# Input projections in three f32r passes over rounded high and low parts, in units of 128 columns, with spilled features and alternating heads

## The reference

```python
h_lat = modulate(rmsnorm(x_lat, norm_mix_g[l]), mod[0], mod[1])     # h_ctx alike
# layer 0, even_mixer
z = h_lat @ w_in                        # (1024 x 3104): bg cg xa q g | k v lr_f lr_b
la_f = log_sigmoid(lr_f @ decay_up[0] + decay_b[0]) / GLA_TAU       # la_b alike
o, _, _ = gla_bidir(q * scale, k, v, la_f, la_b, s_f, s_b)          # 4 heads, chunks of 64
conv = dwconv(cg * xa, conv_w, conv_b, 1)
y = concatenate([bg * conv, gla_readout(o, g, norm_g)]) @ w_out
# layer 1, odd_mixer
xb, gb, u, v = split(h_lat @ w_in)      # 4 x 512 columns
xc = dwconv(xb, conv_w, conv_b, 2)      # then two gates, and a scan in either direction
y = concatenate([(h_f + h_b) * gelu(gb), gelu(u) * mixed(layernorm(gelu(v)))]) @ w_out
# both layers
x = x + mod[2] * y;  x = x + mod[5] * ec_moe(modulate(rmsnorm(x, norm_ffn_g[l]), mod[3], mod[4]))
```

## Time and profile before

| | us |
|---|---|
| median of the runs | 2886.24 (2885.51 to 2896.28, 3 runs) |
| profiled execution | 2893.62 |
| its span | 2891.9 |
| TensorE busy | 2593.5 (90%) |
| VectorE busy | 1715.7 (59%) |
| ScalarE busy | 1364.0 (47%) |
| mean granted TensorE clock | 0.92 |

### The profile page before, as it was taken

How to read it: one execution, slowest core, us unless ns; L and a number is a source line. 1 busy time by engine, 2 the same in 40 slices (tenths; PEclk the granted TensorE clock), 3 DMA queues, 4 the chain that set the end, 5 groups by cost and what they waited for, 6 DMA issues and landing times.

```text
span 2891.9 us, 30954 instructions
## 1 busy us (share of the span) xinstructions
PE 2593.5 (90%) x11696; PEld 1733.4 (60%) x11696; DVE 1715.7 (59%) x1903; ACT 1364.0 (47%) x1371; POOL 182.6 (6%) x210
## 2 busy tenths in 40 slices
PE   4999999888897699999999995999888399999995
PEld 2444445476584366666666664544467278888884
DVE  3130020333456488888888873354554799999995
ACT  4210000144452466666666654155434277777774
POOL 0000000000000110101111000000000001111100
PEclk6899999877897799999999996999998699999997
DMA  6003332200246477878787874101134399999995
GB/s 223 29 0 116 116 115 89 73 16 1 88 175 230 173 270 288 301 280 306 281 308 280 292 251 133 44 0 44 58 132 167 130 361 388 392 391 391 391 376 200
DMA packets 164503, 571.02 MB, mean 197 GB/s; under 512 B 13640, under 2 KB 36928, under 8 KB 158272
## 3 DMA queue, kind: packets, MB, share of 16 engines
q1 hardware_dynamic: 153664, 532.07, 49.0%
q0 software_dynamic: 10752, 37.75, 5.2%
HBM read 527.84 MB, written 41.94 MB: 197 GB/s over the span
## 4 chain that ended last, share of the span: by engine, by line
PE 84%; DVE 6%; DMA 4%; ACT 3%; issue 1%; SPq 0%; POOL 0%; POOLq 0%; ACTq 0%; DVEq 0%
PE ps L541 17%; PE ps L1391 13%; PE ps L1392 12%; PE ps L1393 12%; PE ps L1404 6%; PE ps L551 4%; PE ps L682 3%; PE ps L743 2%; PE ps L745 2%; PE ps L744 2%; PE ps L472 1%; DMA R_W<-in_ada_w 1%; PE ps L758 1%; PE ps L1412 1%; PE ps L1476 1%
## 5 line engine op out<-in xcount | busy, mean ns | idle before, releaser
L1603 DVE TENSOR_TENSOR R_H_r<-R_M,R_W_r 128x2048 fp32r<-128x2048 f32 x336 | 761.8, 2289 | 147.2 <-ACT R_W_r L1506 146.9
L1506 ACT CAST R_W_r<-R_M 128x2048 fp32r<-128x2048 f32 x336 | 640.3, 1913 | 221.2 <-PE ps L1393 82.5
L1393 PE MATMUL ps<-R_W_r,R_C_r 128*128 128x512 f32 x1536 | 607.4, 395 | 0.0
L541 PE MATMUL ps<-R_H,R_W 128*128 128x512 f32 (+1 forms) x1408 | 533.6, 539 | 2.1 <-ACT R_W L1894 1.3
L541 PEld LDWEIGHTS ps<-R_H,R_W 128*128 128x128 f32 x1408 | 267.8, 191 | 273.1 <-issue 256.0
L1391 PE MATMUL ps<-R_W_r,bc_r 128*128 128x512 f32 x1024 | 413.4, 404 | 13.0 <-DVE R_C_r L1621 9.5
L1392 PE MATMUL ps<-R_H_r,bc_r 128*128 128x512 f32 x1024 | 405.8, 396 | 0.0
L1393 PEld LDWEIGHTS ps<-R_W_r,R_C_r 128*128 128x128 f32 x1536 | 291.3, 190 | 65.5
L1391 PEld LDWEIGHTS ps<-R_W_r,bc_r 128*128 128x128 f32 x1024 | 194.1, 190 | 70.7 <-issue 16.4
L1392 PEld LDWEIGHTS ps<-R_H_r,bc_r 128*128 128x128 f32 x1024 | 194.3, 190 | 41.5
L1391 PE MATMUL ps<-R_W_r,R_M_r 128*128 128x512 f32 x512 | 202.6, 396 | 7.0 <-DVE R_C L1693 4.6
(11 more groups left out here) (253 smaller groups left out, 2886.4 us busy)
## 6 DMA issues: line engine op xcount, KB each, us to landing
R_M<-in_moe_w_gate SPq DMA_DIRECT2D x114, 1024.0 KB, 7.9
R_M<-in_moe_w_down SPq DMA_DIRECT2D x112, 1024.0 KB, 7.3
R_M<-in_moe_w_up SPq DMA_DIRECT2D x110, 1024.0 KB, 7.3
R_W<-in_ada_w SPq DMA_DIRECT2D x48, 1024.0 KB, 6.6
R_H<-in_moe_w_up SPq DMA_DIRECT2D x18, 1024.0 KB, 9.5
R_H<-in_moe_w_down SPq DMA_DIRECT2D x16, 1024.0 KB, 9.9
R_H<-in_moe_w_gate SPq DMA_DIRECT2D x14, 1024.0 KB, 9.5
R_W<-in_ev_w_in SPq DMA_DIRECT2D x12, 1024.0 KB, 7.0
```

What stands on the lines that cost most here:

```text
L541: ins = pe.matmul(wide(j % 2, n)[:, c0:c0 + cn], w[:, k, half * P:(half + 1) * P], hT[:, k, c0:c0 + cn], start=(k == 0), stop=(k == KC - 1))
L1393: ins = pe.matmul(o, lo[:, k, 0:P], wh[:, kk, cs], start=False, stop=(k == KC - 1))
L1506: nc.scalar.copy(whi[j], raw[slot + j]).then_inc(unit_high_done, 1)
L1603: nc.vector.tensor_tensor(wlo[j], raw[slot + j], whi[j], ALU.subtract).then_inc(unit_low_done, 1)
```

## The change

Both layers' input projections now run as the output projection does. ScalarE copies a weight unit of 128 columns into f32r (`act_weight_high`), VectorE subtracts that from the raw one in place (`dve_weight_low`). h is modulated and rounded by ScalarE into R_H (`act_h_high`), and VectorE computes it again and subtracts (`dve_h_low`), so its low part stands in R_C. A job is then three f32r matmuls for each k and stretch. R_C being taken, the finished features (bg, g) go into scratch rows and from there to DRAM on GpSimd's queue, and come back as a whole after the last job.

What comes with it: v is made in two halves of 256 columns; the low-rank job is an ordinary job on 128 columns; the first eight ada units go into seven slots in R_M and are computed between the norm's transposes, x is loaded on ScalarE's queue into R_H at once, and the norm writes unmodulated copies of 512 columns. The other 24 ada units of the stage use one slot, two to a job, behind its first and second stretch. The order of the 18 late jobs becomes cg, xa, bg, twice, g, q. The exps and decays of head pair 0 stand ahead of the last jobs. In the attention, the loop over the heads is the inner one. In layer 1, gb goes to `bc` and u to the ends of R_H and R_C, the gate weights are loaded per channel group by ScalarE, and `fill` has 16 half tiles. The MoE and the output projection keep their instructions.

```diff
+        raw_at = [0, PIECE, 2 * PIECE, 6 * PIECE]
+        high_at = [3 * PIECE, 4 * PIECE, 5 * PIECE, 7 * PIECE]
+        wraw = [R_W[:, a:a + PIECE] for a in raw_at]
+        whigh = [R_Wr[:, a:a + PIECE] for a in high_at]
+        wlow = [R_Wr[:, a:a + PIECE] for a in raw_at]
...
+        even_units = [("lr", E_LR + 2 * RANK - P, 0), ("k0", E_K, 1), ("k1", E_K + P, 2), ("v3", E_V + 3 * P, 3),
+                      ("v0", E_V, 0), ("v1", E_V + P, 1), ("v2", E_V + 2 * P, 2)]
+        even_late = [(n, h + i, c + (h + i) * P) for h in (0, 2) for n, c in (("cg", E_CG), ("xa", E_XA), ("bg", E_BG)) for i in range(2)]
+        even_late += [("g", i, E_G + i * P) for i in range(4)] + [("q", i, E_Q + i * P) for i in range(2)]
+        even_units += [(f"{n}{b}", col, i % 3) for i, (n, b, col) in enumerate(even_late)]
+        odd_units = [("xb0", O_XB, 0), ("xb1", O_XB + P, 1), ("xb2", O_XB + 2 * P, 2), ("xb3", O_XB + 3 * P, 0),
...
+            group, place = i // 6, 2 * (i % 6) + part
+            if place < KC:
+                return "unit", N_FIRST + KC * group + place
+            return ("rows", 1 + group) if place == 9 else (None, None)
...
+        fill = [[("v", i) for i in range(6)], [("v", 6), ("v", 7), ("gb", 0)],
+                [("v", i) for i in range(8, 14)], [("v", 14), ("v", 15), ("gb", 1)],
+                [("gb", 2)], [("gb", 3), ("u", 0)], [("u", 1)], [("u", 2), ("u", 3)]]
...
+        split_behind = {("xb", 0): ["xb3"], ("xb", 1): ["w0"], ("xb", 2): ["w1"], ("xb", 3): ["gb0"], ("v", 7): ["w2", "w3"],
+                        ("gb", 0): ["gb1"], ("v", 15): ["gb2", "gb3"], ("gb", 1): ["u0"], ("gb", 2): ["u1"],
+                        ("gb", 3): ["u2"], ("u", 0): ["u3"]}
...
-            unit_in(pe, i)
-            w = ring[slot_of[i]].rearrange("p (k n) -> p k n", k=KC)
-            for c0, cn in SPLIT:
+            pe.wait_ge(weight_low_done, u + 1)
+            wh = whigh[slot_of[u]].rearrange("p (k n) -> p k n", k=KC)
+            wl = wlow[slot_of[u]].rearrange("p (k n) -> p k n", k=KC)
+            for part, (c0, cn) in enumerate(SPLIT):
                 if c0 >= n:
                     break
+                o = wide(j % 2, n)[:, c0:c0 + cn]
                 for k in range(KC):
-                    ins = pe.matmul(wide(j % 2, n)[:, c0:c0 + cn], w[:, k, half * P:(half + 1) * P],
-                                    hT[:, k, c0:c0 + cn], start=(k == 0), stop=(k == KC - 1))
+                    if h_from is not None:
+                        pe.wait_ge(h_low_done, h_from + KC * part + k + 1)
+                    pe.matmul(o, wh[:, k, :], tokens_of(R_Hr, k, c0, cn), start=(k == 0), stop=False)
+                    pe.matmul(o, wh[:, k, :], tokens_of(R_Cr, k, c0, cn), start=False, stop=False)
+                    ins = pe.matmul(o, wl[:, k, :], tokens_of(R_Hr, k, c0, cn), start=False, stop=(k == KC - 1))
+                if part < 2 and beside is not None:
+                    what, at = gap_ada(beside, part)
+                    if what == "unit":
+                        if at == N_FIRST:
+                            pe.wait_ge(v_tile_copied, 2 * NT)
+                        ada(pe, at)
+                    elif what == "rows":
+                        ada_rows(pe, at)
             ins.then_inc(job_done, 1)
...
+            vh, vl = pair_of(high_at, s), pair_of(raw_at, s)
+            o = ps[:, 6 + x % 2, 0:256].rearrange("p (u n) -> p u n", u=2)
             for k in range(KC):
-                ins = pe.matmul(out_, hT[:, k, t * P:(t + 1) * P], v2[:, k, :, :],
-                                start=(k == 0), stop=(k == KC - 1))
+                xh, xl = tokens_of(R_Hr, k, t * P, P), tokens_of(R_Cr, k, t * P, P)
+                pe.matmul(o, xh, vh[:, k, :, :], start=(k == 0), stop=False)
+                pe.matmul(o, xh, vl[:, k, :, :], start=False, stop=False)
+                ins = pe.matmul(o, xl, vh[:, k, :, :], start=False, stop=(k == KC - 1))
...
             for t in range(NT):
                 norm_transposes(pe, t, 2 * (t % 2), t - 2 if t >= 2 else None)
+                if t < N_FIRST:
+                    ada(pe, t)
+            ada_rows(pe, 0)
...
+            for j in range(3):
+                job(pe, j, j, h_from=0 if j == 0 else None)
+            j = 3
...
+            for x in range(2 * NT):
+                half, t = divmod(x, NT)
+                if t == 0:
+                    pe.wait_ge(weight_low_done, max(index["v0"], index["v1"]) + 1 if half == 0 else index["v2"] + 1)
+                if x >= 2:
+                    pe.wait_ge(v_tile_copied, x - 1)
+                v_tile(pe, x, t, 2 * half)
+            for i in range(len(even_late)):
+                job(pe, j, index["cg0"] + i, beside=i)
+                j += 1
             assert j == n_even_jobs
...
-                    for hh in range(2):
-                        for r in range(2):
-                            for tt in range(2):
+                    for r in range(2):
+                        for tt in range(2):
+                            for hh in range(2):
...
-                    for hh in range(2):
-                        for tt in range(2):
-                            t = 2 * g + tt
-                            o = ps[:, 6 + hh, tt * P:(tt + 1) * P]
-                            vh = vtok[:, t, (2 * p + hh) * P:(2 * p + hh + 1) * P]
-                            mm = [(o, vh, attS[:, n % 2, r, (2 * hh + tt) * P:(2 * hh + tt + 1) * P]) for r in range(2)]
-                            for r in range(2):
-                                for cc in range(2):
-                                    c = 2 * t + cc
-                                    if c != order[r][0]:
-                                        qd = (qT if r == 0 else kT)[64 * hh:64 * hh + 64, p, c * 64:(c + 1) * 64]
-                                        mm.append((o[:, cc * 64:(cc + 1) * 64], SIN[64 * hh:64 * hh + 64, r, c, :], qd))
-                            for x, (oo, lhs, rhs) in enumerate(mm):
-                                ins = pe.matmul(oo, lhs, rhs, start=(x == 0), stop=(x == len(mm) - 1))
+                    for tt in range(2):
+                        t = 2 * g + tt
+                        for r in range(2):
+                            for hh in range(2):
+                                pe.matmul(ps[:, 6 + hh, tt * P:(tt + 1) * P],
+                                          vtok[:, t, (2 * p + hh) * P:(2 * p + hh + 1) * P],
+                                          attS[:, n % 2, r, (2 * hh + tt) * P:(2 * hh + tt + 1) * P],
+                                          start=(tt == 0 and r == 0), stop=False)
+                    carried = [(r, c) for c in range(4 * g, 4 * g + 4) for r in range(2) if c != order[r][0]]
+                    for r, c in carried:
+                        for hh in range(2):
+                            qd = (qT if r == 0 else kT)[64 * hh:64 * hh + 64, p, c * 64:(c + 1) * 64]
+                            ins = pe.matmul(ps[:, 6 + hh, (c % 4) * 64:(c % 4 + 1) * 64], SIN[64 * hh:64 * hh + 64, r, c, :],
+                                            qd, start=False, stop=((r, c) == carried[-1]))
...
+        def act_h_high(act, l, n0):
+            act.wait_ge(tile_normed, n0 + NT)
+            act.wait_ge(h_written_by_vector, n0 + NT)
+            act.wait_ge(h_written_by_scalar, n0 + NT)
+            act.wait_ge(scales_done, (1, 3)[l])
+            for c0, cn, k in MODULATED:
+                sc_, sh_ = columns(l, 0, k, c0 // P)
+                nc.scalar.activation(tokens_of(R_Hr, k, c0, cn), tokens_of(R_C, k, c0, cn), ACT.Identity,
+                                     bias=sh_, scale=sc_).then_inc(h_high_done, 1)
+        def dve_h_low(dve, own, l):
+            done = len(MODULATED) * l
+            last = None
+            for i, (c0, cn, k) in enumerate(MODULATED):
+                sc_, sh_ = columns(l, 0, k, c0 // P)
+                x = tokens_of(R_C, k, c0, cn)
+                dve.wait_ge(h_high_done, done + i + 1)
+                full = own.mark(nc.vector.tensor_scalar(x, x, sc_, sh_, ALU.mult, ALU.add))
+                if last is not None:
+                    dve_h_rest(dve, *last)
+                last = (full, c0, cn, k)
+            dve_h_rest(dve, *last)
+        def dve_h_rest(dve, full, c0, cn, k):
+            dve.wait_ge(vector_own, full)
+            nc.vector.tensor_tensor(tokens_of(R_Cr, k, c0, cn), tokens_of(R_C, k, c0, cn), tokens_of(R_Hr, k, c0, cn),
+                                    ALU.subtract).then_inc(h_low_done, 1)
+        def act_weight_high(act, u):
+            act.wait_ge(unit_loaded[slot_of[u]], 16 * n_in_slot[u])
+            nc.scalar.copy(whigh[slot_of[u]], wraw[slot_of[u]]).then_inc(weight_high_done, 1)
+        def dve_weight_low(dve, u):
+            dve.wait_ge(weight_high_done, u + 1)
+            nc.vector.tensor_tensor(wlow[slot_of[u]], wraw[slot_of[u]], whigh[slot_of[u]],
+                                    ALU.subtract).then_inc(weight_low_done, 1)
...
```

(60 more changed lines are left out.)

500 lines of the change are left out of this document (259 added, 241 removed).

## The result

The changed kernel takes **2751.91 us** (2750.12 to 2752.91, 4 runs) where the kernel before took 2891.26 beside it on the same chip. The ratio is 0.9517, its interval 0.9491 to 0.9543. That is 139 us less.

The account below looks back on a forecast made before the run. TensorE, busy 90% of the span, was taken as the bound, with its idle stretches and low clock. Terms -7 - 66 - 6.6 - 24 + 14 = -90 us gave 2796 us on the median, range 2758 to 2836.

Parts of the forecast that it names:

- 0.120 us for the short record: Projections: an f32r matmul record with 256 columns and a new weight tile takes 0.120 us, its load hidden.
- -66 us: The 18 late projection jobs, up to 560.7 us before: their stage takes 276 us against 342.8.
- Rival 1: Projections: short records cost 0.150 us, the load only half hidden; +38, so 2834 us; chance 0.12.
- Rival 2: Projections: short records' loads not hidden, 0.191 or 0.213 us each; 2886 or 2913 us; chance 0.04.
- Rival 4: Late jobs: the single ada slot is late, 2 us on each of 12 jobs, 2816 us; chance 0.20 shared with two others.
- -7: Start to the end of the values: ends at 211 us against 217.8; bounds +15 and -15.
- about 2.0 + 1.9 us per tile on a cold TensorE, so the norm ends near 55 to 58: Start, norm stage: transposes plus ada units at that pace for 10 tiles from about 21 us.
- -30.6: Whole attention stage: 6.6 us from exps and decays moved ahead of the last job, 24 from its loop.
- from 8.67 to about 6: Attention loop: a group's period in us at full clock, as records of different heads alternate.
- ten groups, some at 1.2 GHz: -24, bounds 0 and -35: Attention loop: the shorter group period saves 24 us over ten groups, some of them at the low clock.
- Rival 3: Attention gains nothing, its clock low throughout; 2820 us; chance 0.20 shared with two others.
- +14: Layer 1: up to xb3's end 4 us longer, the eight items about 10 for the clock; bounds -10 and +30.

Follow-up runs that it names:

- the warm pairs: Head pairs at full clock in the two runs with nine unread 512-column matmuls ahead of the scores: 44.9 us in the old order, 29.9 in the new.
- the warm start in the kernel before: Kernel before plus nine unread 512-column matmuls in the state stage ahead of the attention scores: 2889.54 us, ratio 0.9984.
- the warm start in the kernel after: Changed kernel plus nine unread 512-column matmuls in the state stage ahead of the attention scores: 2747.59 us, ratio 0.9504.

## Why the prediction was right or wrong

**The matmul's price and the late jobs: right.** 0.120 us for the short record and -66 us held (0.1195 to 0.120, -65.2). Rivals 1, 2 and 4 are out. The step that carried it was to take the overhead of 0.0136 us from the 512-column records and to check the load against 16-column ones.

**The start: -7 became -22.** The step that failed is "about 2.0 + 1.9 us per tile on a cold TensorE, so the norm ends near 55 to 58". A tile took 2.07 us and the stage ended at 43.05. I carried the clock of the kernel before into a stage whose gaps the change removed. The runs show that the stage needs x early (26 us more without, part of it the way those loads are issued) and that interleaving with ada does nothing (1.5 us): ScalarE and VectorE set its pitch. What kept the clock up in this stage is not isolated. Behind the norm the steps held: the paced job took 23 us as forecast. The 6 us for v2's transfer were 3.9.

**The attention: -30.6 became -58.** The exps ahead of the last job gave 6.4 of 6.6. The period's forecast, "from 8.67 to about 6", was good, and ends at 5.72. What failed is the step from period to stage, "ten groups, some at 1.2 GHz: -24, bounds 0 and -35". It left out that the full matmuls cost 0.16 us each only because of the changes between 128 and 64 rows, and it let the clock speak for a smaller gain alone ("stays low longer because the work is thinner"). The clock was up 8 and 10 us after a pair's first scores instead of 25 and 24, and didn't fall again within the groups. Rival 3, the attention gaining nothing, is the opposite of what happened. Of the other 51.6 us, 30 are the order at full clock, as the warm pairs show, some 19 the clock, and 2.5 lie outside the groups. Why the new order brings the clock back sooner stays open.

**Layer 1: +14 became +2.** The mechanism was right; the steps that were mis-sized are the norm stage's 33 us, the time to xb3's end and the 220 us of the items. TensorE waited 25.1 us ahead of xb0 (I had 23 plus a cold start), and it waited for the gelu in items 0 and 2, 22.3 us (I had 22). The norm stage took 29.5 us where I made it 33, and xb3 was out 111.3 us after the first transfer where I had 116; the items with their clock took 213.4 us where I had 220. ScalarE's waits for weight units were at most 3.1 us each, 13.4 in all, since these land in 4 us rather than the 5 to 6 that I had.

The three misses make 54 us towards faster; the late jobs (0.8) and the rest (1.3) take 2 back. That is the 52 us by which the profiled execution's -142 stands below the forecast's -90.

## What to carry to other kernels

When a change fills the gaps of a stage, price that stage at the clock that the filled stage will have, and ask in which order matmuls of different height follow each other: the same records cost half when neighbours lie on different rows of the array. Where one queue's transfers take turns with the work, compare the transfer under load (6 to 9 us here) with the stage's pitch (2 us) before believing in the double buffer. And look for what stands between a short wait and its cause on the releasing engine: weight parts of about 1 us stood behind a pass of 22 us here, and TensorE waited 25 us for them.

## What was not expected of the hardware

- TensorE shown as busy for 30 us, with its loads busy for some 86% of it, can stay at 1.2 GHz (600 to 630 us of the warm start in the kernel before, granted 0.50), after a fall from 1.00. The same order of matmuls kept 1.00 for 45 us one pair of heads later (677 to 722 us). With the new order such a fall lasted 3 us (554 to 557 us of the warm start in the kernel after).
- Full 128x128 records and 64-row ones start 0.112 us apart within a block of their kind, and 0.20 us apart at a change from one kind to the other. So a full one costs 0.16 us in blocks of four among 64-row ones and 0.117 in a block of 16.
- Two 64-row records on different rows of the array start within 0.007 us of each other; on the same rows they start 0.11 us apart.
- A 256-column f32r record with a new weight tile has a pitch of 0.120 us, so its load is wholly hidden, with load records that say 0.19 us.
- 0.5 MB of x took 5.9 to 8.7 us beside the other loads of the start and 3.2 without. A weight unit of 0.5 MB in rows of 512 B landed in 3.9 us.
